# Seven block products on token tiles in the down projections of a two-block network, one NeuronCore

## What is computed

```python
x = layer_norm(x, ln0_g, ln0_b)
for l in range(DEPTH):
    mix = hybrid_mixer(x, w_in[l], ...)
    x = layer_norm(alpha * x + mix, ln1_g[l], ln1_b[l])
    hid = jnp.square(jax.nn.relu(jnp.einsum('bsd,df->bsf', x, w_up[l])))
    x = layer_norm(alpha * x + jnp.einsum('bsf,fd->bsd', hid, w_down[l]), ln2_g[l], ln2_b[l])
```

```python
mod = jax.nn.silu(c) @ ada_w[i] + ada_b[i]          # ada_w[i]: 1024 x 6144
mod_c = jax.nn.silu(c_ctx) @ ada_w[i] + ada_b[i]
```

## Time and profile before

| | us |
|---|---|
| median of 3 runs | 2590.72 (2590.28 to 2592.64) |
| the profiled execution, its own time | 2589.31 |
| its span in the profile | 2587.5 |
| TensorE busy | 2531.8 |
| VectorE busy | 1426.7 |
| ScalarE busy | 532.6 |
| GpSimd busy | 317.3 |

### The profile page before, as it was taken

How to read it: one execution, slowest core, us unless ns; L and a number is a source line. 1 busy time by engine, 2 the same in 40 slices (tenths; PEclk the granted TensorE clock), 3 DMA queues, 4 the chain that set the end, 5 groups by cost and what they waited for, 6 DMA issues and landing times. The chain is left out here.

```text
span 2587.5 us, 38626 instructions
## 1 busy us (share of the span) xinstructions
PE 2531.8 (98%) x16192; PEld 1964.6 (76%) x16192; DVE 1426.7 (55%) x2632; ACT 532.6 (21%) x1249; POOL 317.3 (12%) x367
## 2 busy tenths in 40 slices
PE   8999999999999999999999999999998999999998
PEld 7888886864688898687468757888886656666997
DVE  1575454865247454483456825555434378863775
ACT  1342220100135121011012921000003143321000
POOL 2001111210100121031000000000000145510110
PEclk9999999999999999999999999999999999999999
DMA  7331114887533211488742012222222434434552
GB/s 265 114 117 64 43 59 147 302 283 249 174 122 115 83 35 51 143 282 293 252 167 82 18 33 86 94 82 79 84 86 72 146 114 127 131 98 151 167 171 106
DMA packets 253603, 341.80 MB, mean 132 GB/s; under 512 B 7252, under 2 KB 179412, under 8 KB 253304
## 3 DMA queue, kind: packets, MB, share of 16 engines
q1 hardware_dynamic: 241632, 311.71, 36.4%
q10 hardware_dynamic: 8920, 17.67, 2.1%
q0 software_dynamic: 2880, 9.96, 1.1%
HBM read 338.13 MB, written 1.19 MB: 131 GB/s over the span
## 5 line engine op out<-in xcount | busy, mean ns | idle before, releaser
L1000 PE MATMUL PS<-MEM 128*128 128x256 f32 (+1 forms) x2632 | 448.0, 332 | 2.6 <-ACT MEM L1418 1.2
L1000 PEld LDWEIGHTS PS<-MEM 128*128 128x128 f32 x2632 | 406.4, 190 | 43.8 <-issue 1.9
L397 PE MATMUL PS<-MEM 128*128 128x256 f32 x1632 | 356.5, 379 | 5.1 <-DMA MEM<-w_up 5.1
L1377 ACT ACTIVATE MEM<-PS 128x256 f32<-128x256 f32 (+4 forms) x405 | 167.3, 428 | 916.0 <-PE PS L397 226.8
L397 PEld LDWEIGHTS PS<-MEM 128*128 128x128 f32 x1632 | 308.4, 190 | 48.3 <-DMA MEM<-w_up 5.9
L443 PE MATMUL PS<-MEM 128*128 128x512 f32 x608 | 263.4, 593 | 5.4 <-POOL MEM L2907 3.2
L1983 DVE SCALAR_TENSOR_TENSOR MEM<-MEM 128x512 f32<-128x512 f32 x280 | 218.0, 811 | 57.3 <-DMA MEM<-ada_w 51.2
L443 PEld LDWEIGHTS PS<-MEM 128*128 128x128 f32 x608 | 114.8, 190 | 150.2 <-issue 140.8
L2857 POOL TENSOR_TENSOR MEM<-MEM 128x1 f32<-128x1 f32 (+1 forms) x34 | 21.8, 643 | 1264.6 <-DVE MEM L1929 807.0
L669 PE MATMUL PS<-MEM 128*128 128x256 f32 x768 | 172.3, 382 | 0.0
L1274 PE MATMUL PS<-MEM 128*128 128x512 f32 (+1 forms) x512 | 170.2, 485 | 0.0
(11 more groups left out here) (377 smaller groups left out, 3257.9 us busy)
## 6 DMA issues: line engine op xcount, KB each, us to landing
MEM<-w_in SPq DMA_DIRECT2D x54, 1024.0 KB, 5.3
MEM<-ada_w SPq DMA_DIRECT2D x48, 1024.0 KB, 7.3
MEM<-w_up SPq DMA_DIRECT2D x32, 1024.0 KB, 5.4
MEM<-w_down SPq DMA_DIRECT2D x32, 1024.0 KB, 5.1
MEM<-ssm_w_in SPq DMA_DIRECT2D x24, 1024.0 KB, 5.3
MEM<-ffn_gate SPq DMA_DIRECT2D x22, 1024.0 KB, 5.2
MEM<-ffn_up SPq DMA_DIRECT2D x22, 1024.0 KB, 5.2
MEM<-ffn_down SPq DMA_DIRECT2D x20, 1024.0 KB, 5.0
```

Of the source, the lines that this page charges most:

```text
L397: ins = pe.matmul(bank[:, 0:T], W[:, k, c * P:(c + 1) * P], XT[:, k, :], start=k == 0, stop=k == KT - 1)
L1000: ins = pe.matmul(out, left[:, k, :], right[:, k, :], start=k == 0, stop=k == 3)
L1377: act.activation(out, view(b), func, **kw).then_inc(S("bank_read_by_act"), 1)
```

## The change

The down projections of the first block are now made by `down_first` instead of `wide`. A half (512 columns) is seen as 2 x 2 blocks: token tiles of 128 tokens, pairs of hidden tiles, and column blocks of 256. Over a pair of hidden tiles (f) the four output blocks come from seven products of 128x256 instead of eight: p1 and p2 of plain operands, the others with sums and differences of hidden tiles (`HSUM1`) or of weight blocks (`DS1`) or of both. A slab has two pairs, so 14 products. They add up in six banks over the eight slabs of a half.

- GpSimd makes the sums of the hidden tiles: behind the two squares of a pair four operations of 128x128 (one in place in `HID`).
- GpSimd makes the sums of each weight slab (`weights`): four operations of 128x512, two of them behind a wait for the one before, into one of two sets `DS1`. A set is written again when TensorE has used it (`first_sums_used`). Slabs 0 and 1 are summed behind the last two pairs of hidden tiles, the others later in the stage.
- TensorE takes p1, p2, p3 of a slab, waits for its sums (`first_summed`), then takes p6, p7, p5, p4. For the last two slabs of a half p2 and p3 are put at the end. The weight slab's place is free after its p4.
- ScalarE copies p1 out of its bank (F1), VectorE combines the others in `first_tile` and `second_tile` with 128x256 additions, in place of `residual`. Token tile 0 is complete after p4, tile 1 after p2 and p3.
- The conditioning groups are 12 and 12 slabs (`ADA_GROUP`) in place of 18 and 6: one `ada_products` ahead of the down projection, one behind it. `ACC` holds 12 slabs, and VectorE waits with the 13th until the first product has been made.
- GpSimd's loads for the next layer come after the weight sums. `ACC` and `AROW` lie elsewhere.

```diff
+            def down_first(w, l):
+                x, y = slice(P, 2 * P), slice(0, P)
+                ca, cb = slice(0, T), slice(T, 2 * T)
+                last = NFIRST - 1
...
+                                "p1": (HID[:, 2 * f, x], W[j][:, 2 * p, ca]),
+                                "p2": (HID[:, 2 * f + 1, x], W[j][:, 2 * p + 1, ca]),
+                                "p3": (HSUM1[:, f, 2, :], W[j][:, 2 * p + 1, cb]),
+                                "p4": (HID[:, 2 * f + 1, y], ds[3][:, p, :]),
+                                "p5": (HSUM1[:, f, 0, :], ds[0][:, p, :]),
+                                "p6": (HSUM1[:, f, 1, :], ds[1][:, p, :]),
+                                "p7": (HID[:, 2 * f, y], ds[2][:, p, :])}[name]
...
+                    for j in range(NFIRST):
+                        if j < ADA_DOWN:
+                            ada_slab()
+                        W[j] = b_slab(w, 4 * j, 512 * half)
...
+                        pe.wait_ge(S("hid_summed"), 2 * NFIRST * l + 2 * (j + 1))
+                        if j < last - 1:
+                            for name in ("p1", "p2", "p3"):
+                                product(name, j)
...
+                        pe.wait_ge(S("first_summed"), NFIRST * (2 * l + half) + j + 1)
+                        for name in ("p6", "p7", "p5", "p4"):
...
+                            if j < last - 1:
+                                close_slab(("first_sums_used", last * (2 * l + half) + j + 1))
+                    for name in ("p2", "p3"):
+                        product(name, last - 1)
+                        done(product(name, last))
...
-                pe.wait_ge(S("hid_squared"), (DFF // P) * (l + 1))
-                wide(w_down[l], lambda k, t: HID[:, k, t * P:(t + 1) * P], DFF // P, lambda h, t: ("dn", l, h, t), between=True, by_token=True,
...
-                ada_turned(ADA_DOWN + ADA_UP)
-                ada_products(ADA_DOWN)
+                ada_products(ADA_GROUP)
+                down_first(w_down[l], l)
+                if l < DEPTH - 1:
+                    turn_tile(n0 + 2, 0, turn_banks(n0 + 2, 0))
+                ada_turned(ADA_GROUP)
+                ada_products(ADA_GROUP)
...
-                ada_sums(ADA_UP + ADA_DOWN)
+                ada_sums(ADA_UP)
+                peek(dve, ("modrow", 24 * l))
+                ada_sums(ADA_DOWN)
...
+                def weights(i):
...
+                    W = RING[:, at % NSLOT, :].rearrange("p (k n) -> p k n", k=4)
+                    b11, b12, b21, b22 = [W[:, j:4:2, c:c + T] for j in range(2) for c in (0, T)]
+                    q = DS1[i % 2]
+                    pool.tensor_tensor(q[2], b22, b12, ALU.subtract)
+                    pool.tensor_tensor(q[0], b12, b11, ALU.subtract).then_inc(S("first_sum_step"), 1)
+                    pool.wait_ge(S("first_sum_step"), 2 * n + 1)
+                    pool.tensor_tensor(q[1], b22, q[0], ALU.subtract).then_inc(S("first_sum_step"), 1)
+                    pool.wait_ge(S("first_sum_step"), 2 * n + 2)
+                    pool.tensor_tensor(q[3], b21, q[1], ALU.subtract).then_inc(S("first_summed"), 1)
```

More of the change, by code:

```diff
@@ L289, in build @@
         SC = SM[:, 353:369].rearrange("p (k t) -> p k t", k=KT)
-        ACC = mem(9, 2, 512, at=part)
-        AROW = mem(256, at=part + 9216)
+        HSUM1 = mem(DFF // (2 * P), 3, P, at=keep + 8192)
+        ACC = mem(ADA_GROUP // 2, 2, 512, at=keep + 14336)
+        AROW = mem(256, at=keep + 20480)
+        DS1 = [[mem(2, T, at=R1 + 4368 if (b, j) == (1, 3) else keep + 20736 + 512 * (4 * b + j)) for j in range(4)] for b in range(2)]
+        F2, F3 = [mem(T, at=R2B + 254 + 256 * i) for i in range(2)]
+        F1, F4, FA, FB = [mem(T, at=R2B + 1024 + 256 * i) for i in range(4)]
         assert part + 12032 <= 53200
@@ L345, in build @@
         narrow_at = []
+        first_at = []
+        NFIRST = DFF // (4 * P)
         seven_at = []
@@ L411, in _, with wide @@
             used = [0]
-            def wide(w, src, nk, keyf, nt=NT, between=None, second=None, by_token=False, midway=None, turn=None):
+            def wide(w, src, nk, keyf, nt=NT, second=None, by_token=False, turn=None):
                 for half in range(2):
@@ L422, in wide @@
                         n = min(4, nk - k0)
-                        if between and s < ADA_DOWN:
-                            ada_slab()
                         W = b_slab(w, k0, 512 * half, n)
@@ L453, in wide @@
                             second()
-                    if between and half == 0:
-                        ada_products(ADA_DOWN + ADA_UP)
-                        if midway:
-                            midway()
             def turn_normed(n, which=None):
@@ new lines, in second_tile @@
+                def second_tile(half, ca, part):
+                    b = filled(dve, "dve", ("d", l, 4 + part, half))
+                    c, own = ((FA, F1), (FB, F4))[part]
+                    read(dve.tensor_tensor(c, b[:, 0:T], own, ALU.add))
+                    settle()
+                    return added(1, ca, c)
+                ca, cb = slice(0, T), slice(T, 2 * T)
+                first_tile(0, ca, cb)
+                second_tile(0, ca, 0)
+                link(second_tile(0, cb, 1))
@@ L2912, in _ @@
+                if l == DEPTH - 1:
                     for t in RMS_TILES[0][:NT]:
                         power(MS2[:, t:t + 1])
+                for i in range(NFIRST, 2 * NFIRST):
+                    weights(i)
                 for t in range(NT):
```

134 lines of the change are left out of this document (105 added, 29 removed).

## The result

The changed kernel takes 2626.52 us (median of 4 runs, 2624.37 to 2627.71) against 2590.77 us for the kernel before on the same chip: ratio 1.0133, 95% interval 1.0121 to 1.0145. It is 35.7 us slower, where the prediction's sum gave 8.8 us. The time is 20 us above the 2592 to 2606 us of the forecast proper, and half a microsecond above the upper end of the whole range (2626 us). The profiled execution took 2626.61 us, its span is 2624.8 us.

What follows compares the result with a forecast made beforehand. TensorE, busy 2531.8 of 2587.5 us, was taken to bound the kernel. First layer +13.9 and second -5.1 us made +8.8 us, on the 2590.72 us median 2599 us; range 2578 to 2626 us.

Steps and rivals of the forecast that it cites:

- forecast proper: Whole kernel: the prediction's own case, 2592 to 2606 us, chance 0.50.
- Products: Down projections: 128 products of 0.8625 us become 224 of 0.433 us in each layer, -26.9 us for both.
- Hidden tiles' sums and the start: Before the down stages: GpSimd's small sums stay hidden; the wait for the last squares goes, -1.5 and -1.7 us.
- Price of a GpSimd operation: Down stages: each 128x512 weight sum on GpSimd takes about 0.72 us from VectorE, bounds 0.35 and 1.09 us.
- whole operation: Rival, down stages: a GpSimd operation shuts VectorE out for all of its 1.09 us; 2623.5 us, chance 0.20.
- The first layer's sum: Down stage: VectorE needs 8.4 us a conditioning slab, 62.5 us a half against 55.2, +14.6 us; layer +13.9.
- The second layer: Down stage: the weight slabs' ring is the bound, 53.5 us a half against 55.2, -3.4 us; layer -5.1.
- the ring's loop: Second layer's weight slabs: landing, GpSimd's sums, eight products and handovers take 13.8 us for two slabs, 6.9 each.
- GpSimd's own queue is passed by nothing urgent: GpSimd's DMA queue: small loads for the next layer's low-rank weights stand behind the sums, some 70 us before use.
- Ends: Layer ends: tile 0's transposes wait 0.8 us in the first layer; the second layer's end costs nothing, given its slack.

Runs made afterwards that it cites:

- e2: Changed kernel with GpSimd's weight sums one column wide and p4 to p7 on plain weight blocks: 2574.22 us, ratio 0.9937 to the kernel before.
- e8: Changed kernel with GpSimd's two layer-norm row loads moved back to the start of the up projection: 2630.6 us, ratio 1.0149 to the kernel before.
- e9: Changed kernel with three extra, unread TensorE products ahead of each wait for sums in the first layer: 2626.74 us, ratio 1.0134 to the kernel before.
- e11: Changed kernel with slab 6 of each down projection's first half taken in plain order: 2628.17 us, ratio 1.0139 to the kernel before.
- e1: Changed kernel with VectorE making only one operation of each conditioning slab in the down stages: 2601.97 us, ratio 1.0038 to the kernel before.
- e4: Changed kernel with the weight sums made by VectorE instead of GpSimd: 2593.97 us, ratio 1.0008 to the kernel before.
- e12: Changed kernel with first layer's down projection plain, second's sums on VectorE, first-half slab 6 plain, row loads mid up projection: 2581.7 us, 0.9961 of the kernel before.

## Why the prediction was right in sign and wrong in size

**Products.** Right: rows that follow one another without a stop cost what the earlier trace rows says (60 rows from 619.12 in 13.22 us, 0.220 us each); without its sums the kernel gains 17 us (e2).

**Hidden tiles' sums and the start.** Right. The wait for the last squares is gone, and the up projection's 448 rows take 96.86 us without a wait.

**Price of a GpSimd operation.** The mechanism was right, the size was not: 0.93 us instead of 0.72. I took the earlier trace rows as they stood, and their GpSimd operation is 1.09 us alone, where the sums are 1.26 us alone; the turn in which VectorE passes one operation grew from 1.42 to 1.65 us, and what is lost is the turn less VectorE's own 0.73. It lies between my forecast and the rival "whole operation" (1.09), whose time, 2623.5 us, and whose half of 71.5 us (measured: 71.8 and 72.2) came closest. That is luck: by its mechanism VectorE would lose all of a 1.26 us operation, and a part of the measured halves is made by terms that neither sum has (below). That the range reached close to the measured time is owed to this rival; the forecast itself ended at 2606 us.

**The first layer's sum.** Forecast 125.0 us for the down stage (2 x 62.5), measured 143.9. VectorE's rows account for the 18.9 us, by one term that was sized wrong and three that my sum lacked:
- VectorE's twelve slabs take 15.4 + 41.1 + 54.1 = 110.6 us, not 12 x 8.4 = 100.8, by the price: 9.8 us.
- VectorE waits 3.1 us for its third slab (572.94), since the loads of the rows meet it (gone in e8): 3.1 us.
- At the half's change VectorE adds up the six banks, from 621.25 on, before it takes the next slab. Before, there was room for that; now it begins the slab at 629.26, 3.2 us after TensorE has ended the half at 626.05 (32 of the 60 rows from 619.12 belong to it, at 0.2165 us). 3.2 us.
- After VectorE's last slab (683.4) come a landing, the sums of slabs 6 and 7 and the last products: 14.9 us to the end, not 2 x 6.06 = 12.1. 2.8 us.

That is 18.9 us. The waits of TensorE (8.49 us at 575.67 among them) are no terms of their own, as e8, e9 and e11 suggest: they are what is left of TensorE's time when VectorE and the ring set the pace. Below VectorE's pace lies the ring's: without VectorE's part the stage still takes 118.9 us (e1). I had looked for the cause in them first.

**The second layer.** Forecast -5.1 us, measured +9.9. The bound that I named, the ring's loop, fits what the runs show, and its size was wrong. Three of SyncE's issues in the second half, and the first and the last sum and the products of the slab that is issued at 1312.19:

```profile
1312.19 0.37 SPq L3135 DMA_DIRECT2D MEM<-w_down  x1
...
1320.08 0.37 SPq L3135 DMA_DIRECT2D MEM<-w_down  x1
...
1328.09 0.37 SPq L3135 DMA_DIRECT2D MEM<-w_down  x1
...
1317.48 1.78 POOL L3026 TENSOR_TENSOR MEM<-MEM 128x512 f32<-128x512 f32 x1 [1.21 <-DMA MEM<-w_down]
...
1322.69 1.59 POOL L3031 TENSOR_TENSOR MEM<-MEM 128x512 f32<-128x512 f32 x1
...
1324.34 6.31 PE L496 MATMUL PS<-MEM 128*128 128x256 f32 x28 [1.69 <-POOL MEM L3031]
```

From 1312.19, the issue, to 1317.48 the slab lands (5.3 us); the sums last until 1324.28 (6.8); eight products take 3.5 us; the next issue into this place is at 1328.09, after 15.9 us for two slabs. The loop one slab later (1320.08 to 1335.05) takes 15.0 us. I had 5.1 + 5.0 + 3.5 + 0.2 = 13.8. In these two loops the term that was sized wrong is the sums: 5.0 us from the 1.09 of the earlier trace rows, 6.8 measured. At 7.5 to 8.0 us a slab the seven products lose to the 6.9 us of before. If these loops stood for all 12 slabs, this would make 7 to 13 us, an estimate; 4.0 us of waiting for a slab at 1263.54 (rows and context are loaded there) and 2.4 us at the half's change for VectorE come on top. That is 14 to 20 us for the 16.2 that the down stage is above its forecast (125.1 against 2 x 53.5 and 1.9 for transposes).

How the 16 us divide stays open, though. In e1 the sums have their own length and a loop of the second half takes 14.5 us (issues at 1288.82 and 1303.29), yet the stage takes 123.9 us: what VectorE adds to the sums is worth 1.2 us here. For the rest there are a sum's own 1.26 us, the slab that meets the loads (issued at 1251.53, landed 12.0 us later) and the half's change; no run parts them. That the step between landing and product is what the stage hangs on, e4 and e12 show: with sums of 0.69 us it takes 107.0 and 104.5 us.

**"GpSimd's own queue is passed by nothing urgent".** Wrong: I looked at the loads for the low-rank weights and missed those of the layer norms' rows, which went into the stage's busiest place. By e8 it cost nothing in sum, since something came back that I had not forecast either: the up projections' waits of 2.71 us and 2.35 us for w_up, with which the loads had met before, fell to nothing and 0.22 us.

**Ends.** 0.67 us for tile 0's transposes at the first layer's end, forecast 0.8. In the second layer some 1 us more than forecast: TensorE waits 1.66 us there, 0.54 before, for ScalarE's copy of a conditioning product.

The Trainium skill (SBUF — State Buffer, section Who interferes with whom) has the kind of conflict right, and says that issue order decides who blocks. e1 agrees that the pair of engines costs the time: without VectorE's part 24.5 us come back. The section calls the shared ports an exclusive lock, and writes of the full block for the whole instruction where it speaks of VectorE's two-port modes. For the operations here a full block is not what the trace shows: both engines go on, in turns of 1.65 us for 1.26 + 0.73 us of work.

The Trainium skill (GPSIMD Engine Reference, section 3.1, Elementwise — side-by-side cycle accounting) gives 4497 ns for 2048 columns of a two-operand addition; an estimate from it for 512 columns is 1.12 us. The earlier trace rows agree, with 1.09 us. The sums of this change take 1.26 us, 0.14 more.

## What to carry to other kernels

Before moving operations on two buffer operands to GpSimd beside a busy VectorE, compare what they take from VectorE there (here 0.93 us) with what they cost on VectorE itself (0.69 us); if the first is more, an idle GpSimd is no help. Compare also what they add between a landing and its use (1.26 us or more against 0.69). A cheaper form of the same products pays only where the ring, with its added step between landing and product, still turns faster than the products, and where the engine beside has room: here in the second layer, not in the first. And when several engines wait for each other, follow the one that idles least within the stage (VectorE, in the first layer here); filling, moving or removing the waits of the others changed nothing in three runs.

## What was not expected of the hardware

- The same form and shape of GpSimd operation took 1.09 us at one place and 1.26 us at another, both alone; neither the operands' pattern nor the operation explains it.
- Each stop of TensorE shows about 0.25 us beyond the wait: 28 rows of the seven products between two stops take 6.31 us, where the earlier trace rows give 28 x 0.2165 = 6.06 for an unbroken run. (The profile models the ends of matmuls.)
- In the wait of 8.49 us TensorE's granted clock fell to the lower of its two levels (1.2 of 2.4 GHz) and stayed there for 10.2 us; the first 12 rows behind the wait took 5.49 us instead of 2.86. It was there for 30.7 us in the whole stage, in which TensorE has waits every few microseconds, and cost nothing that could be measured (e9), since another engine set the end.
